# Dropping TensorE's constant multiplications from a 256-token, six-FFN network in split fp32

## The chip, the cores and the metric

The kernel runs on one core of one Trainium2 chip. The metric is device time in microseconds, the median of several executions. A core has TensorE (PE: matmuls, and PEld for its weight loads), VectorE (DVE), ScalarE (ACT), GpSimd (POOL) and SyncE (SP), each with its own in-order queue, coupled by semaphores.

## The reference

Two networks in a row act on x of 256 tokens by 1024 features, all in fp32:

```python
# first_block, DEPTH = 2
for i in range(DEPTH):
    x = layer_norm(ALPHA * x + 0.5 * swiglu(x, ...), ...)
    x = layer_norm(ALPHA * x + (mixer_ab or mixer_c)(x, ...), ...)
    x = layer_norm(ALPHA * x + memory_attn(x, mem, ...), ...)
    x = layer_norm(ALPHA * x + 0.5 * swiglu(x, ...), ...)
# second_block, DEPTH = 2
for l in range(DEPTH):
    h = _rmsnorm(x, mix_norm[l])
    x = x + _mixer(h, ...)      # gated delta rule and HGRN2, both directions
    h = _rmsnorm(x, ffn_norm[l])
    x = x + _conv_ffn(h, ...)
return _rmsnorm(x, final_norm)
```

The mixer of the second block computes merged = sigmoid(gate_dn) * (o_dn @ w_branch_dn) + sigmoid(gate_hg) * (o_hg @ w_branch_hg), and returns merged @ w_out. The constant multiplications of the kernel appear nowhere in it.

## The kernel before, in words

All weights come in one stream of "units" of 128 x 2048 values (1 MB), by SP into a ring of three. ACT rounds each half unit to fp32r (w_hi, L1272), DVE (in some stages POOL, L2528) subtracts to get the rest (ring_lo, L1690), and PE multiplies three times: high by high, high by low, low by high. features (L714) makes one unit into one PSUM tile of two 128 x 256 halves, 48 matmuls with 256 moving columns (L724); tokens (L728) does the same with the roles exchanged; to_acc (L744) adds one unit into the four PSUM banks acc, 24 matmuls of 512 columns (L757). There are four rotating tile banks; open_tile (L687) waits until the bank's earlier tile was taken.

There are six FFNs, 0 to 3 in the first block, 4 and 5 in the second. A norm works on the finished acc banks: DVE adds them to x and takes statistics (L1769 and L1770, for RMS norms L2054 and L2055), ACT takes a square root, DVE normalizes the rows in two instructions (L1780, for RMS norms L2064; each adds 1 to the semaphore ln_xh), PE transposes them in 16 records (transposes, L772), ACT and DVE scale them out of PSUM, and ACT L1251 and DVE L1678 split them into xT_hi and xT_lo, which the first features wait for (await_x, L712). Norms 0 to 5 of the first block have two units of the memory's keys and values as work for PE (norm_filled, L817). The norm 6 before FFN 3 and the four RMS norms 0 to 3 go through norm_transposes (L806).

mixer2 (L1052) is run twice. After its projections come LEVELS + 2 = 9 levels (0 to 8): each has a gate unit (none at level 8), a wait for hg_k and hg_q (made by DVE L2214 and POOL L2559), and two tiles of 128 x 128 products (per_head, L1039). Then come the sums for the l2 norms, the decay tables (ACT L1613), a wait for l2_inv ahead of four more tiles, the transposes, seven rounds of a block inverse, the recurrence, the products with the branch weights (branch, L1190, matmuls in L1201), and the output projection (out_proj, L833), whose first to_acc waits for the merged operand.

keep_warm (L693 to L697) multiplies the identity by 512 columns of the constant table, n times, into a bank that later work overwrites; nobody reads the product. Its calls stand in norm_transposes (five times, L807), in out_proj (twice, L835), at level 0 (five times) and level 8 (four times, L1072), before l2_inv (three times, L1114) and before branch_dn (twice, L1210). Each of the five calls stands in PE's order just ahead of a wait. out_proj is used by the second block alone; so the places that are run are 5 norms, and 5 in each of the two layers' mixers.

Of the kernel before, what the change touches and what calls it, by code (L numbers as in the profile page):

```python
# [56 lines left out]
LEVELS = 7  # L57
# [400 lines left out]
def build(nc, weights, x_in, mem_in, consts, cols, ln_g_rows, ln_b_rows, gains, sink, rpb, hmask_in, wba_in, head_rows, decay_rows, final_norm,  # L458
          out):
    plan = Plan()  # L460
    with ExitStack() as ctx:
        def sb(name, shape, dt=F32):
            return ctx.enter_context(nc.sbuf_tensor(name, shape, dt))
# [16 lines left out]
        const = sb("const", [P, CONSTANTS_W])  # L480
# [41 lines left out]
        def table(name):  # L522
            a, n = CONSTANTS[name]
            return const[:, a:a + n]

        ident = table("ident")
# [19 lines left out]
        acc = [ctx.enter_context(nc.psum_tensor(f"acc{b}", [P, 512], F32)) for b in range(4)]  # L546
# [137 lines left out]
        def _(pe):  # L684
            mm = nc.tensor.matmul

            def open_tile(t, more=0):  # L687
                if t >= NB:

                    pe.wait_ge(tile_taken[t % NB], more + t // NB)  # L690
                return bank[t % NB]

            def keep_warm(ps, n):  # L693


                for _ in range(n):
                    mm(ps[:, :], ident, const[:, 0:512], start=True, stop=True)  # L697

            THREE = ((0, 0), (0, 1), (1, 0))
            x2 = (xT_hi, xT_lo)  # L700
            mem2 = (mem_hi, mem_lo)
# [12 lines left out]
            def features(u, t, x_set=None, more=0, x2=x2):  # L714

                for f in range(2):
                    w = open_half(u, f, KT, more)
                    if f == 0:
                        ps = open_tile(t, more)
                    for k in range(KT):  # L720
                        if x_set is not None and f == 0 and k % 2 == 0:
                            await_x(x_set, k // 2)
                        for i, (a, b) in enumerate(THREE):
                            j = mm(ps[:, f * S:(f + 1) * S], w[a][:, k, :], x2[b][:, k, :],  # L724
                                   start=(k == 0 and i == 0), stop=(k == KT - 1 and i == 2))
                    j.then_inc(sems["unit_used" if f else "half_used"], 1)
# [38 lines left out]
            def transposes(t0, src):  # L765

                for q in range(4):
                    ps = open_tile(t0 + q)
                    for k in range(2):
                        for tt in range(TT):  # L770
                            c = (2 * q + k) * P
                            i = nc.tensor.transpose(ps[:, k * S + tt * P:k * S + (tt + 1) * P],  # L772
                                                    src[:, tt, c:c + P], ident)
                    i.then_inc(sems["tile_ready"], 1)

            def await_features(t0):
                for q in range(4):
                    pe.wait_ge(*taken(t0 + q))
# [24 lines left out]
                    transposes(plan.tile["mem"], mem_rows)  # L803
                down(FT // 2 - 1, u0 + FU - 1, False, True)

            def norm_transposes(key, inst, warm=5):  # L806
                keep_warm(open_tile(plan.tile[key]), warm)  # L807
                pe.wait_ge(sems["ln_xh"], 2 * (inst + 1))
                transposes(plan.tile[key], xh)
                await_features(plan.tile[key])  # L810
# [17 lines left out]
            def out_unit(n, j):  # L828

                await_x(("out", n), j)  # L830
                to_acc(plan.unit[("out", n, j)], x2, 2 * j, j == 0, j == 3)

            def out_proj(n):  # L833

                keep_warm(acc[0], 2)  # L835
                for j in range(4):
                    out_unit(n, j)

# [180 lines left out]
            norm_filled(5)  # L1019
            memory_attention(1)  # L1020
            norm_transposes(("ln", 6), 6)
            ffn(3, ("ln", 6))

# [11 lines left out]
            def per_head(t, lhsT, rhs, part=lambda out: out):  # L1035

                ps = open_tile(t)
                for h in range(4):
                    i = mm(part(ps[:, h * P:(h + 1) * P]), lhsT(h), rhs(h), start=True, stop=True)  # L1039
                i.then_inc(sems["tile_ready"], 1)  # L1040

            def hd(h):
                return slice(h * P, (h + 1) * P)

            def turn4(t, src):

                ps = open_tile(t)
                for b in range(4):
                    i = nc.tensor.transpose(ps[:, b * P:(b + 1) * P], src(b), ident)
                i.then_inc(sems["tile_ready"], 1)  # L1050

            def mixer2(l):  # L1052
                U, T = plan.unit, plan.tile
# [14 lines left out]
                for i in range(LEVELS + 2):  # L1068
                    if i < 8:
                        features(U[("gate", l, i)], T[("gate", l, i)])  # L1070
                    if i in (0, LEVELS + 1):
                        keep_warm(open_tile(T[("level", l, i)]), 5 if i == 0 else 4)  # L1072
                    pe.wait_ge(sems["hg_k"], (LEVELS + 2) * l + i + 1)
                    pe.wait_ge(sems["hg_q"], (LEVELS + 2) * l + i + 1)
                    K, Q = hKQ[:, i % 2, 0], hKQ[:, i % 2, 1]
                    for c in range(2):
                        s, t = (c, c) if i <= LEVELS else (c, 1 - c)
                        per_head(T[("level", l, i)] + c,
                                 lambda h: K[:, h * S + s * P:h * S + (s + 1) * P],
                                 lambda h: Q[:, h * S + t * P:h * S + (t + 1) * P])  # L1080

                pe.wait_ge(sems["l2_sq"], 4 * l + 4)
                ps = open_tile(T[("l2", l)])
                for c in range(16):
                    i = mm(ps[:, c:c + 1], l2s[:, c // 2, (c % 2) * P:(c % 2 + 1) * P], table("ones")[:, 0:1],  # L1085
                           start=True, stop=True)
# [4 lines left out]
                for tt in range(TT):  # L1091
                    ps = open_tile(T[("hg_o", l)] + tt)
                    for h in range(4):
                        for st in range(TT):
                            i = mm(ps[:, hd(h)], hatt[:, st, h, tt * P:(tt + 1) * P], hi[:, st, hd(h)],  # L1095
                                   start=(st == 0), stop=(st == TT - 1))
# [3 lines left out]
                ps = open_tile(T[("gcum", l)])  # L1100
# [5 lines left out]
                i = mm(ps[:, 16:32], table("ones"), gg[:, :], start=True, stop=True)  # L1106
# [4 lines left out]
                             lambda h: gg[:, tt * 8 + d * 4 + h:tt * 8 + d * 4 + h + 1].to_broadcast([P, P]),  # L1111
                             lambda h: sums[d])

                keep_warm(acc[0], 3)  # L1114
                pe.wait_ge(sems["l2_inv"], l + 1)
                for j in range(4):
                    per_head(T[("l2B", l)] + j, lambda c: l2i[:, 4 * j + c:4 * j + c + 1].to_broadcast([P, P]),
# [64 lines left out]
                for tt in range(TT):  # L1182
                    pe.wait_ge(*taken(T[("QK", l)] + tt))
                    ps = open_tile(T[("dn_o", l)] + tt)
                    for h in range(4):
                        for d in range(2):
                            i = mm(ps[:, hd(h)], qkd[:, 2 * tt + d, hd(h)], vn[:, 2 * tt + d, hd(h)],  # L1187
                                   start=(d == 0), stop=(d == 1))
                    i.then_inc(sems["tile_ready"], 1)
                def branch(name, q0):  # L1190

                    for j in range(2):
                        for half in range(2):
                            w = open_half(U[(name, l)] + j, half, 4)
                            ps = open_tile(T[(name, l)] + 2 * j + half)
                            for f in range(2):
                                for k in range(4):
                                    if j + half + f == 0 and k % 2 == 0:
                                        await_x(("branch", l), q0 + k // 2)
                                    for p, (c, d) in enumerate(THREE):  # L1200
                                        i = mm(ps[:, f * S:(f + 1) * S], w[c][:, k, f * P:(f + 1) * P],  # L1201
                                               x2[d][:, 2 * q0 + k, :], start=(k + p == 0), stop=(k == 3 and p == 2))
                            i.then_inc(sems["unit_used" if half else "half_used"], 1)
# [3 lines left out]
                pe.wait_ge(sems["dn_out"], l + 1)  # L1207
                for j in range(2):
                    turn4(T[("dn_T", l)] + j, lambda b: dn_o[:, b % 2, hd(2 * j + b // 2)])
                keep_warm(acc[0], 2)  # L1210
                branch("branch_dn", 2)
                out_proj(4 + l)

            pe.wait_ge(sems["head_in"], 16 * 2)
            for l in range(DEPTH):
                norm_transposes(("rms", 2 * l), 8 + 2 * l)
                mixer2(l)
                norm_transposes(("rms", 2 * l + 1), 9 + 2 * l)
                ffn(4 + l, ("rms", 2 * l + 1))
# [1412 lines left out]
```

## Time and profile before

| | |
|---|---|
| median of 3 runs | 2501.81 us (2498.66 to 2504.06) |
| the profiled execution | 2507.15 us |
| its span, first to last instruction | 2505.3 us |
| mean granted TensorE clock | 0.963 |
| PE busy | 2325.2 us, 93% |
| DVE busy | 1661.1 us, 66% |
| ACT busy | 1057.3 us, 42% |
| DMA | 359.80 MB, mean 144 GB/s |

The clock is given as a share of full speed: 1.00 is 2.4 GHz, 0.50 is 1.2 GHz. In a timeline row the columns are start, duration, engine, line and operation, then output and inputs; a bracket tells how long the engine was idle before it and who ended that. Each fp32 matmul with fp32 operands appears as two records; those of the three-part products (fp32r) appear as one. The ends of PE's records are modelled, so neighbours overlap; their starts are the better measure.

### The profile page before, as it was taken

The numbers are of one execution on the slowest core, as the hardware profiler recorded it, in microseconds if no ns is written. First come the engines' busy times: TensorE is split into PE (matmuls) and PEld (weight loads), VectorE is DVE, ScalarE is ACT, GpSimd is POOL, SyncE is SP. The second block draws the span as 40 slices with busy tenths as digits, with TensorE's granted clock in tenths as the row PEclk, the third lists the DMA queues.
The fourth block names the chain that finished last, engine by engine and source line by source line (L and its number), as shares of the span: only waits on it lengthen the run. The fifth ranks groups of instructions, "written<-read, shape, count | busy, mean of one in ns | idle before, by whom it ended". The sixth has DMA issues, their size and how long they took to land. (4 is left out here: it accounts for less than half of the span.)

```text
span 2505.3 us, 40714 instructions
## 1 busy us (share of the span) xinstructions
PE 2325.2 (93%) x16414; PEld 2162.1 (86%) x16414; DVE 1661.1 (66%) x2425; ACT 1057.3 (42%) x1481; POOL 309.2 (12%) x192
## 2 busy tenths in 40 slices
PE   7999789989999999999979887999999887899997
PEld 7999659879999997989969877988998887897997
DVE  4557656665665567665567886467666988547766
ACT  4335445433443456543335444234444443324432
POOL 0000000320000000000003353400000544320000
PEclk9999889989999999999989898999999998899999
DMA  6555314755455543445535320024554332003553
GB/s 258 187 186 178 109 48 155 189 180 185 178 201 187 188 161 120 158 153 186 186 119 185 119 100 34 1 89 164 185 184 165 139 117 85 1 18 144 187 184 132
DMA packets 52674, 359.80 MB, mean 144 GB/s; under 512 B 6401, under 2 KB 6785, under 8 KB 10945
## 3 DMA queue, kind: packets, MB, share of 16 engines
q1 hardware_dynamic: 46928, 340.81, 37.9%
q0 software_dynamic: 4336, 13.37, 1.9%
q10 hardware_dynamic: 1280, 3.77, 0.4%
q8 instruction: 97, 1.59, 0.3%
q14 instruction: 33, 0.26, 0.0%
HBM read 356.88 MB, written 1.05 MB: 143 GB/s over the span
## 5 line engine op out<-in xcount | busy, mean ns | idle before, releaser
L1690 DVE TENSOR_TENSOR ring_lo<-ring,w_hi 128x1024 fp32r<-128x1024 f32 x600 | 758.0, 1294 | 616.4 <-ACT w_hi L1272 614.7
L1272 ACT ACTIVATE w_hi<-ring 128x1024 fp32r<-128x1024 f32 x648 | 656.2, 1052 | 875.7 <-DMA ring<-weights 726.2
L724 PE MATMUL tile<-xT_hi,w_hi 128*128 128x256 f32 x3008 | 863.1, 287 | 38.3 <-DVE ring_lo L1690 24.4
L724 PE MATMUL tile<-xT_lo,w_hi 128*128 128x256 f32 x3008 | 858.7, 285 | 0.0
L724 PE MATMUL tile<-xT_hi,ring_lo 128*128 128x256 f32 x3008 | 858.3, 285 | 0.0
L724 PEld LDWEIGHTS tile<-xT_hi,w_hi 128*128 128x128 f32 x3008 | 585.4, 195 | 45.5 <-DVE ring_lo L1690 30.9
L724 PEld LDWEIGHTS tile<-xT_lo,w_hi 128*128 128x128 f32 x3008 | 585.5, 195 | 2.1
L724 PEld LDWEIGHTS tile<-xT_hi,ring_lo 128*128 128x128 f32 x3008 | 584.7, 194 | 0.0
L1039 PE MATMUL tile<-work 128*128 128x128 f32 (+1 forms) x1600 | 201.1, 290 | 43.9 <-DVE work L2214 40.5
L1039 PEld LDWEIGHTS tile<-work 128*128 128x128 f32 x1600 | 195.5, 204 | 51.7 <-DVE work L2214 45.8
L757 PE MATMUL acc<-w_hi,hidden_hi 128*128 128x512 f32 x528 | 208.1, 394 | 5.7 <-DVE ring_lo L1690 5.6
L1237 ACT ACTIVATE work<-tile 128x512 f32<-128x512 f32 (+1 forms) x204 | 112.6, 574 | 228.3 <-PE tile L1039 120.0
L757 PE MATMUL acc<-w_hi,hidden_lo 128*128 128x512 f32 x528 | 207.5, 393 | 0.0
L757 PE MATMUL acc<-ring_lo,hidden_hi 128*128 128x512 f32 x528 | 206.6, 391 | 0.0
L2528 POOL TENSOR_TENSOR ring_lo<-ring,w_hi 128x1024 fp32r<-128x1024 f32 x48 | 133.8, 2797 | 469.6 <-ACT w_hi L1272 469.6
L757 PEld LDWEIGHTS acc<-w_hi,hidden_hi 128*128 128x128 f32 x528 | 100.2, 190 | 26.0 <-issue 6.0
L2502 POOL DMA_DIRECT2D work<-ln_g_rows x8 | 4.4, 555 | 937.1 <-DVE x L1791 936.8
L757 PEld LDWEIGHTS acc<-ring_lo,hidden_hi 128*128 128x128 f32 x528 | 99.9, 189 | 21.5
L757 PEld LDWEIGHTS acc<-w_hi,hidden_lo 128*128 128x128 f32 x528 | 100.1, 190 | 18.4
L737 PE MATMUL tile<-w_hi,xT_hi 128*128 128x256 f32 x352 | 102.5, 291 | 5.0 <-DVE work L1914 2.8
L737 PE MATMUL tile<-w_hi,xT_lo 128*128 128x256 f32 x352 | 101.9, 290 | 0.0
L737 PE MATMUL tile<-ring_lo,xT_hi 128*128 128x256 f32 x352 | 101.7, 289 | 0.0
(259 smaller groups left out, 3027.5 us busy)
## 6 DMA issues: line engine op xcount, KB each, us to landing
ring<-weights SPq DMA_DIRECT2D x324, 1024.0 KB, 4.8
work<-ln_g_rows POOLq DMA_DIRECT2D x8, 512.0 KB, 5.5
work<-ln_b_rows POOLq DMA_DIRECT2D x8, 512.0 KB, 6.7
work<-rpb POOLq DMA_DIRECT2D x32, 96.0 KB, 14.0
work<-hmask_in ACTq DMA_DIRECT2D x1, 1408.0 KB, 9.9
x<-x_in SPq DMA_DIRECT2D x1, 1024.0 KB, 8.0
work<-mem_in ACTq DMA_DIRECT2D x1, 1024.0 KB, 7.0
out<-x POOLq DMA_DIRECT2D x1, 1024.0 KB, 4.4
```

Of the source, the lines that this page charges most:

```text
L724: j = mm(ps[:, f * S:(f + 1) * S], w[a][:, k, :], x2[b][:, k, :], start=(k == 0 and i == 0), stop=(k == KT - 1 and i == 2))
L737: j = mm(ps[:, tt * 256:(tt + 1) * 256], x2[b][:, k, tt * P:(tt + 1) * P], w[k // 4][a][:, k % 4, :], start=(k == 0 and i == 0), stop=(k = ...
L757: j = mm(acc[b][:, :], src[d][:, at + k, (b // 2) * P:(b // 2 + 1) * P], w[k][c][:, 0, (b % 2) * 512:(b % 2 + 1) * 512], start=(first and ...
L1039: i = mm(part(ps[:, h * P:(h + 1) * P]), lhsT(h), rhs(h), start=True, stop=True)
L1237: A(dst, ps[:, :] if src is None else src(ps), ACT.Copy).then_inc(tile_taken[t % NB], 1)
L1272: A(high_of(u, h), half_of(ring, u, h), ACT.Copy).then_inc(sems["w_hi"], 1)
L1690: V.tensor_tensor(half_of(ring_lo, u, h), half_of(ring, u, h), high_of(u, h).bitcast(F32), ALU.subtract).then_inc(sems["w_lo"], 1)
L2502: pool.dma_start(g_rows, ln_g_rows[inst:inst + 1, :].partition_broadcast(P)).then_inc(sems["rows_in"], 16)
L2528: G.tensor_tensor(half_of(ring_lo, u + 2, h), half_of(ring, u + 2, h), high_of(u + 2, h).bitcast(F32), ALU.subtract).then_inc(sems["w_lo_p ...
```

## The change

The function keep_warm and its five calls are removed; the parameter warm of norm_transposes goes with them. Nothing else is changed.

```diff
-            def keep_warm(ps, n):
-
-
-                for _ in range(n):
-                    mm(ps[:, :], ident, const[:, 0:512], start=True, stop=True)
-
...
-            def norm_transposes(key, inst, warm=5):
-                keep_warm(open_tile(plan.tile[key]), warm)
+            def norm_transposes(key, inst):
                 pe.wait_ge(sems["ln_xh"], 2 * (inst + 1))
                 transposes(plan.tile[key], xh)
                 await_features(plan.tile[key])
...
             def out_proj(n):
 
-                keep_warm(acc[0], 2)
                 for j in range(4):
                     out_unit(n, j)
...
                     if i < 8:
                         features(U[("gate", l, i)], T[("gate", l, i)])
-                    if i in (0, LEVELS + 1):
-                        keep_warm(open_tile(T[("level", l, i)]), 5 if i == 0 else 4)
                     pe.wait_ge(sems["hg_k"], (LEVELS + 2) * l + i + 1)
...
-                keep_warm(acc[0], 3)
                 pe.wait_ge(sems["l2_inv"], l + 1)
...
                 for j in range(2):
                     turn4(T[("dn_T", l)] + j, lambda b: dn_o[:, b % 2, hd(2 * j + b // 2)])
-                keep_warm(acc[0], 2)
                 branch("branch_dn", 2)
                 out_proj(4 + l)
```

## Rows read from the trace of the kernel before

**Rows 1.** The page: the span, busy time of engines, and TensorE's granted clock in 40 slices.
```profile
span 2505.3 us, 40714 instructions
...
PE 2325.2 (93%) x16414; PEld 2162.1 (86%) x16414; DVE 1661.1 (66%) x2425; ACT 1057.3 (42%) x1481; POOL 309.2 (12%) x192
...
PEclk9999889989999999999989898999999998899999
```
**Rows 2.** Groups by line, PE: record count | busy us, mean ns | idle before.
```profile
L697 PE MATMUL tile<-const 128*128 128x512 f32 x86 | 38.4, 592 | 0.0
...
L697 PE MATMUL acc<-const 128*128 128x512 f32 x28 | 13.0, 592 | 0.0
```
**Rows 3.** Timeline at norm 6, before FFN 3: start, duration, engine, line.
```profile
1087.25 4.45 PE L697 MATMUL tile<-const 128*128 128x512 f32 x10
...
1089.93 1.53 DVE L1780 TENSOR_SCALAR work<-work,mv,rstd 128x1024 f32<-128x1024 f32 x2
...
1091.54 1.95 PE L772 MATMUL tile<-const,work 128*128 128x128 f32 x16
...
1095.53 0.35 PE L724 MATMUL tile<-xT_hi,w_hi 128*128 128x256 f32 x1 [2.04 <-DVE xT_lo L1678]
```
**Rows 4.** Timeline of PE at RMS norm 1, before FFN 4 (the second RMS norm).
```profile
1699.24 4.45 PE L697 MATMUL tile<-const 128*128 128x512 f32 x10
1703.92 1.97 PE L772 MATMUL tile<-const,work 128*128 128x128 f32 x16 [0.22 <-DVE work L2064]
1707.71 0.35 PE L724 MATMUL tile<-xT_hi,w_hi 128*128 128x256 f32 x1 [1.83 <-DVE xT_lo L1678]
```
**Rows 5.** Timeline of PE in layer 0's levels: behind gate unit 1, and level 8.
```profile
1467.33 2.98 PE L1039 MATMUL tile<-work 128*128 128x128 f32 x15 [4.36 <-DVE work L2214]
...
1529.32 1.01 PE L1039 MATMUL tile<-work 128*128 128x128 f32 x3 [6.34 <-DVE work L2214]
```
**Rows 6.** Timeline of PE behind the wait for l2_inv, layer 0.
```profile
1550.06 1.13 PE L1039 MATMUL tile<-const,small 128*128 128x128 f32 x8 [0.98 <-ACT work L1613]
...
1551.72 1.16 PE L1039 MATMUL tile<-const,small 128*128 128x128 f32 x8 [0.53 <-ACT work L1613]
```
**Rows 7.** Timeline of PE at branch_dn and at out_proj, layer 0.
```profile
1662.03 0.36 PE L1201 MATMUL tile<-xT_hi,w_hi 128*128 128x256 f32 x1 [0.62 <-DVE xT_lo L1678]
...
1677.35 0.50 PE L757 MATMUL acc<-w_hi,xT_hi 128*128 128x512 f32 x1 [1.85 <-DVE xT_lo L1678]
```
**Rows 8.** Stretches: us, busy (count) of PE, PEld, DVE, ACT, POOL; PEclk; DMA.
```profile
1096.10:1099.30 3.20, 3.20 (x17) 3.20 (x16) 3.20 (x4) 2.01 (x3) 0.00 (x0) 0.50 0.02 5
1101.10:1104.30 3.20, 3.20 (x29) 3.20 (x29) 3.17 (x4) 1.43 (x3) 0.00 (x0) 1.00 0.11 20
1307.80:1308.80 1.00, 0.00 (x0) 0.01 (x1) 1.00 (x3) 1.00 (x3) 0.00 (x0) 1.00 0.00 0
1386.00:1387.90 1.90, 0.00 (x0) 0.00 (x0) 1.90 (x5) 1.86 (x2) 0.75 (x1) 1.00 0.42 78
1389.60:1392.80 3.20, 3.20 (x17) 3.20 (x17) 3.17 (x9) 0.00 (x0) 0.61 (x1) 0.50 0.23 90
1396.00:1399.50 3.50, 0.00 (x0) 0.00 (x0) 3.28 (x7) 0.71 (x2) 0.00 (x0) 1.00 0.60 250
1399.80:1403.00 3.20, 2.88 (x13) 2.88 (x14) 3.09 (x8) 1.51 (x2) 1.61 (x1) 0.50 0.03 13
1705.95:1707.70 1.75, 0.00 (x0) 0.02 (x1) 1.67 (x4) 1.75 (x5) 0.00 (x0) 1.00 0.00 0
1707.80:1894.00 186.20, 186.20 (x1317) 175.51 (x1318) 135.52 (x206) 78.66 (x92) 0.00 (x0) 1.00 0.50 181
```
**Rows 9.** Timeline of PE at RMS norm 0, the first, before the mixer of layer 0.
```profile
1303.48 3.67 PE L772 MATMUL tile<-const,work 128*128 128x128 f32 x16 [15.17 <-DVE work L2064]
1308.82 0.36 PE L724 MATMUL tile<-xT_hi,w_hi 128*128 128x256 f32 x1 [1.66 <-DVE xT_lo L1678]
```
**Rows 10.** Source view of line 2064: duration ns min/median/max, first and last start.
```profile
L2064 DVE TENSOR_SCALAR work<-x,rstd x10: 748/751/754, 1302.0 to 2494.8; 128x1024 f32<-128x1024 f32 x10
```

## The prediction

> **What bounds the kernel now.** I read the page first. TensorE (PE) is busy for 93% of a span of 2505.3 us, and its clock row stands at eight or nine tenths throughout [rows 1]. So PE sets the end, and the clock it is granted matters. The profiled execution took 2507.15 us, 1.85 more than its span and 5.3 more than the median of the runs, 2501.81. All terms below are differences within that execution, so I add their sum to either.
>
> Next come the groups by line for what goes away: 86 + 28 records, 38.4 + 13.0 = 51.4 us of busy time, no idle ahead of them [rows 2]. Two records make one fp32 multiplication, so 57 multiplications go, at 0.90 us each. The tempting sum takes 51.4 us off the end. Whether any of it comes off depends, at each place, on what the next PE instruction waits for. So I read the timeline at all 15 places: five norms with transposes of their own, and five in each of the two mixers.
>
> At the norm before FFN 3 the ten records start at 1087.25; VectorE's (DVE's) normalization of both row halves ends at 1089.93 + 1.53 = 1091.46; the transposes start at 1091.54 [rows 3]. At the second RMS norm 0.22 us of idle even stand between the filler and the transposes, ended by DVE L2064 [rows 4]. The next two RMS norms read the same within 0.25 us. In the mixer the idle left behind the fillers is 6.34 us at level 8 [rows 5], 0.98 at l2 [rows 6], and 0.62 at branch_dn and 1.85 at out_proj [rows 7], the same in both layers. Everywhere the release comes last, not the filler.
>
> **The change part by part.** *PE work removed.* The gain per place is the filler's end less the release, at most the 0.1 us of rows 3: nothing in all. What hides this work is the wait itself. The wait inside open_tile that some fillers took is made again by the first transpose or per_head, so no wait moves and nothing queues differently behind one. No DMA and neither SP's nor POOL's queue is touched.
>
> *What follows a silent PE.* Without fillers PE is idle from where they start to the next start: 4.3 us before FFN 3 [rows 3], 4.7 at the second RMS norm [rows 4] (4.4 and 4.7 at the next two). Elsewhere it is the idle left plus 0.90 per multiplication: 3.7 us at l2 (three), 2.4 at branch_dn (two), 3.7 at out_proj (two), about 10 at level 8. The stretches show what such idle brings [rows 8]. After 1.9 us of idle from 1386.0 the next 3.2 us stand at a granted clock of 0.50, that is 1.2 GHz; after 3.5 us of idle from 1396.0 again; after the 2.04 us of idle behind FFN 3's transposes [rows 3] again, at 1096.1. After 1.75 us of idle from 1705.95 FFN 4 ran its 186 us at 1.00 (2.4 GHz). Every idle stretch that the change makes is longer than those 1.9 and 2.04.
>
> *The price of the lower clock.* Of features, 17 fall in 3.2 us at 0.50 and 29 at 1.00 [rows 8]. By these counts such a stretch costs 3.2 x (1 - 17/29) = 1.3 us, by the clock's ratio 1.6; I take 1.5. Sixteen transposes take 3.67 us when PE comes out of a long idle [rows 9] and 1.97 at 1.00 [rows 4]. To the first feature behind them it is 1308.82 - 1303.48 = 5.34 us against 1707.71 - 1703.92 = 3.79, so 1.55 us more. Nothing later absorbs this in an FFN: PE is busy 186.20 of 186.20 us there [rows 8].
>
> *The sum by place.*
> - Norm before FFN 3: its features pay for one slow stretch already; new are slow transposes, 1.5 us (0 to 3).
> - Three RMS norms: slow transposes, 1.55, and part of a stretch of features, up to 1.5. The nearest row, 3.5 us of idle, left the clock low for the first 3.2 us of work, and slow transposes last 3.67, so most is paid there: 2.5 each, 7.5 us (1.55 to 3.05 each).
> - Two branch_dn, idle 2.4, nearest the 1.9 with a fall: 1.5 each, 3.0 us (0 to 3 each).
> - Two out_proj, idle 3.7, nearest the 3.5: 1.5 each, 3.0 us (0 to 3 each).
> - Two l2, idle 3.7: the fall is as likely, but PE then goes in step with ACT, with idle ended by ACT L1613 ahead of each group of eight [rows 6], which absorbs a part; the transposes behind are exposed. 1.0 each, 2.0 us (0 to 4 each).
> - Level 0, two: nothing. Behind the next gate unit PE idles 4.36 us for DVE L2214 [rows 5], and that covers it; without the cover, 1.5 each.
> - Level 8, two, and the first RMS norm: nothing. The idle left there now, 6.34 [rows 5] and 15.17 us [rows 9], brings the clock down before PE resumes.
>
> Sum: 1.5 + 7.5 + 3.0 + 3.0 + 2.0 = 17.0 us. The profiled execution would come to 2524 us, the median to **2519 us**. Late next is whatever PE does behind each place, FFN 4 and 5 above all.
>
> *A rule against the rows.* At the first RMS norm the sixteen transposes were PE's only work since 15.17 us of idle [rows 9], and at 1307.8, before the features began, the clock stood at 1.00 again [rows 8]. So transposes bring it back, and I charge the norms for little behind them.
> The Trainium skill, "TensorE: Matmul & The Clock Gate", Part 4 (PE-mode transpose), says the opposite: in transpose mode the full clock does not engage, since it doesn't count as PE work in the same way. By it each of four norms would pay a further stretch of features. By that rule the third rival follows; this trace disagrees where it shows it.
>
> **The rivals.**
> 1. *No change.* The falls land in idle, or PE's lateness is hidden by what it waits for next. For it: before FFN 3 the clock fell in spite of the fillers [rows 3, 8]. Against it: behind the second RMS norm it did not fall, and there fillers are PE's only work in 4.7 us [rows 4, 8]. With 1 us at each of three RMS norms and nothing else: +3, 2505 us.
> 2. *Faster: the fillers slow the chains that PE waits for.* The place is DVE's and ACT's work beside the fillers, 51.4 us of it; the mechanism, that PE's reads and writes of memory hold theirs up. If those chains grew shorter by a share s, s x 51.4 us comes off: over 33% beats the clock's 17 us, and with the +3 of rival 1, over 6% decides. Against it: the ten executions of DVE's L2064 took 748 to 754 ns, with fillers beside them or not [rows 10]. With a share of 20% and +3: 2495 us.
> 3. *Dearer: the clock comes back late.* The features behind four norms start slow too, 1.5 more each (6 us), and each of the six other places pays two stretches, 3.0 in place of 1.5 or 1.0 (10 us). In all 17 + 16 = 33; with half of the second part, +28, 2530 us. Against it: the row at 1307.8 [rows 8], and that after the slow stretches of rows 8 the rows come back to 1.00 at 1101.1.
> 4. *The change doesn't do what it says:* left aside, since the function and its five calls all go.
>
> **How the numbers follow.** The forecast's case, +6 to +26, gets 0.78, no change (rival 1) 0.09, faster 0.03, dearer than +26 0.10. The range's low end is the sum with branch_dn, out_proj and l2 at nothing and the RMS norms at 1.55 each: 1.5 + 4.65 = +6. The high end is rival 3: +28. That is 2508 to 2530 us. A measurement of this kernel can tell about 0.2%, 5 us, from no change. Slower by more than that gets 0.88, within it 0.09, faster 0.03.
>
> **What would show it right or wrong.** Right: the work behind each wait starts as far behind PE's last work as now (4.3, 4.7, 2.4 and 3.7 us); the transposes of the three RMS norms take 3 to 3.7 us for 16; stretches at 0.50 stand at those places; the mean granted clock falls by some 0.01; the FFNs stay without idle, each starting later. Wrong: if those transposes still take 1.97 us and what is behind them runs at 1.00 (rival 1); if the statistics ahead of L2064 get shorter (rival 2); if features are slow for over 3 us behind slow transposes (rival 3).

## The result, and the profile after

| | before | changed |
|---|---|---|
| median, 7 runs each | 2502.95 us | 2514.74 us |
| ratio | | 1.0049, 95% interval 1.0034 to 1.0065 |
| profiled execution's span | 2505.3 us | 2512.9 us |
| mean granted TensorE clock | 0.963 | 0.952 |
| PE busy | 2325.2 us | 2286.8 us |

The change costs 12.3 us (8.5 to 16.3). PE is busy for 38 us less, and the kernel ends later. A second build of the same changed kernel gave 1.0067 (1.0053 to 1.0081). Microseconds given with a ratio are that ratio less 1, times the median of the kernel before.

These are the page's lines that answer to [rows 1]:

```profile
span 2512.9 us, 40485 instructions
...
PE 2286.8 (91%) x16300; PEld 2153.2 (86%) x16300; DVE 1658.7 (66%) x2425; ACT 1058.6 (42%) x1481; POOL 306.2 (12%) x192
...
PEclk9999889999999999999989888999999988899999
```

PE's other 16300 records are there in both traces in the same order, so a start can be compared with its counterpart. (All line numbers after the removed function are lower now: L766 was L772, L718 was L724, L751 was L757, L1190 was L1201, L1031 was L1039, L2052 was L2064.) The timeline of PE at norm 6, at RMS norms 1 and 2, and at branch_dn and out_proj of the layers 0 and 1, answers to [rows 3, 4, 7]:

```profile
1087.04 3.01 PE L766 MATMUL tile<-const,work 128*128 128x128 f32 x16 [4.11 <-DVE work L1768]
1091.83 0.55 PE L718 MATMUL tile<-xT_hi,w_hi 128*128 128x256 f32 x1 [1.78 <-DVE xT_lo L1666]
...
1660.88 0.36 PE L1190 MATMUL tile<-xT_hi,w_hi 128*128 128x256 f32 x1 [2.33 <-DVE xT_lo L1666]
...
1677.69 0.50 PE L751 MATMUL acc<-w_hi,xT_hi 128*128 128x512 f32 x1 [3.57 <-DVE xT_lo L1666]
...
1705.88 3.47 PE L766 MATMUL tile<-const,work 128*128 128x128 f32 x16 [4.51 <-DVE work L2052]
1711.00 0.35 PE L718 MATMUL tile<-xT_hi,w_hi 128*128 128x256 f32 x1 [1.66 <-DVE xT_lo L1666]
...
1902.50 2.70 PE L766 MATMUL tile<-const,work 128*128 128x128 f32 x16 [4.28 <-DVE work L2052]
1906.86 0.55 PE L718 MATMUL tile<-xT_hi,w_hi 128*128 128x256 f32 x1 [1.66 <-DVE xT_lo L1666]
...
2278.62 0.50 PE L751 MATMUL acc<-w_hi,xT_hi 128*128 128x512 f32 x1 [3.57 <-DVE xT_lo L1666]
```

The idle in the brackets took the place of the fillers to the tenth of a microsecond: at RMS norm 1 the transposes started 4.90 us behind the last acc matmul before and do so now. But they last 3.47 us instead of 1.97, and from their start to the first feature it is 5.12 us instead of 3.79. What the clock did is in the stretches (us; busy and count of PE, PEld, DVE, ACT, POOL; PEclk; DMA):

```profile
1088.00:1091.70 3.70, 2.04 (x10) 1.64 (x8) 2.72 (x7) 3.22 (x7) 0.00 (x0) 0.50 0.00 0
1091.90:1097.20 5.30, 5.30 (x25) 5.30 (x26) 5.30 (x7) 2.32 (x3) 0.00 (x0) 0.50 0.02 3
...
1661.30:1664.50 3.20, 3.20 (x17) 3.20 (x16) 1.18 (x2) 0.00 (x0) 0.00 (x0) 0.50 0.19 77
1678.40:1681.60 3.20, 3.20 (x9) 2.49 (x8) 3.20 (x4) 1.20 (x2) 0.00 (x0) 0.50 0.02 8
1705.70:1708.90 3.20, 3.02 (x14) 3.02 (x15) 2.13 (x4) 1.00 (x3) 0.00 (x0) 0.50 0.01 3
1709.10:1897.80 188.70, 187.04 (x1322) 176.09 (x1321) 137.81 (x209) 80.75 (x96) 0.00 (x0) 1.00 0.50 178
1903.70:1910.30 6.60, 4.94 (x24) 4.57 (x23) 5.87 (x10) 5.14 (x9) 0.00 (x0) 0.50 0.00 0
2259.90:2273.90 14.00, 11.67 (x98) 11.46 (x97) 9.12 (x12) 5.68 (x8) 0.00 (x0) 1.00 0.43 151
```

PE works at 1.2 GHz (0.50) behind nearly every wait that the fillers had covered. At branch_dn of layer 1 (2259.90) the clock stayed at 1.00, though PE had been idle just as long (2.33 us) as at that of layer 0.

The table below is worked out from the traces of all kernels that lack some fillers, as differences of start times: the first column is a part's length in the kernel before, the others how much longer it is. The kernels are described in the next section; **bold** marks a part whose own fillers are missing. "2nd" is a second trace of the same kernel (experiment 10).

| part | before, us | changed | changed, 2nd | norms only | branch and out only | levels and l2 only | all but levels and l2 | before, 2nd |
|---|---|---|---|---|---|---|---|---|
| start to norm 6 (nothing changed) | 1078 | -4.4 | -4.1 | -4.8 | -6.0 | -4.5 | -3.9 | -2.3 |
| norm 6: transposes to first feature | 3.99 | **+0.80** | **+1.17** | 0.01 | **+0.80** | **+1.39** | 0.00 | 0.00 |
| FFN 3, first 14.5 us | 14.52 | **+1.22** | **-1.50** | -1.49 | **+1.22** | **0.00** | 0.00 | -1.49 |
| RMS norm 0: 16 us of features | 16.26 | **+1.47** | **+0.01** | +2.65 | **+1.46** | **+1.42** | 0.00 | +1.42 |
| both layers, level 0 to the l2 products | 218 | **-1.1** | **-2.6** | **-1.6** | **-2.4** | +2.2 | **-2.4** | -1.0 |
| of these, level 0's products to level 1's | 18.35 | **+1.07** | **+1.21** | **+1.65** | **+1.34** | 0.01 | **+1.26** | -0.03 |
| l2 wait and what follows, layer 0 | 24.97 | **+0.01** | **0.00** | **+0.01** | **0.00** | -0.01 | **0.00** | 0.00 |
| branch_dn, layer 0 | 11.46 | **+1.50** | **+1.49** | **+1.49** | 0.01 | **+1.49** | 0.01 | 0.01 |
| branch_dn, layer 1 | 11.47 | **-0.01** | **+1.48** | **+1.48** | -0.01 | **+1.49** | -0.01 | 0.00 |
| out_proj, layer 0 | 21.67 | **+1.62** | **+1.60** | **+1.60** | 0.04 | **+2.41** | 0.04 | 0.04 |
| out_proj, layer 1 | 21.71 | **+1.58** | **+1.57** | **+1.55** | -0.04 | **0.00** | -0.04 | -0.04 |
| RMS norm 1: transposes to first feature | 3.79 | **+1.33** | **+1.37** | 0.00 | **+1.30** | **+1.50** | 0.00 | 0.00 |
| RMS norm 2: transposes and 17 us behind | 20.77 | **+2.12** | **+4.17** | 0.01 | **+1.55** | **+2.83** | 0.01 | 0.02 |
| RMS norm 3: transposes and 14 us behind | 17.79 | **+1.28** | **+1.38** | -0.01 | **+3.38** | **+3.22** | -0.01 | -0.01 |

RMS norm 0's features and the levels as a whole vary as much with their fillers (+1.42 and +2.65; +2.2) as without. Level 0 by itself doesn't: in the five traces without its five multiplications level 1 begins 1.1 to 1.65 us later, both layers together, and in the two others it moves by 0.03 at most. Without them the stretch at half clock there lasts longer (1439.90 to 1446.60 at 0.50 in experiment 4, against 1447.60 to 1450.80 in the kernel before). The other bold parts of the first trace of the changed kernel add up to 0.80 + 1.22 + 0.01 + 1.50 - 0.01 + 1.62 + 1.58 + 1.33 + 2.12 + 1.28 = 11.45 us, nearly the 12.3 of the medians. With level 0's 1.07 they make 12.5. The spans differ by only 7.6, because parts far ahead of the change happened to take 4.4 us less.

### The profile page after: what moved, and what is told of

It reads as the page before. It is cut to its first block and busy times, and to the rows that moved or that the text cites. A ratio compares the mean times of both kernels' runs of the same rounds, so it can differ in the third digit from the quotient of the medians.

```text
span 2512.9 us, 40485 instructions
## 1 busy us (share of the span) xinstructions
PE 2286.8 (91%) x16300; PEld 2153.2 (86%) x16300; DVE 1658.7 (66%) x2425; ACT 1058.6 (42%) x1481; POOL 306.2 (12%) x192
## 3 DMA queue, kind: packets, MB, share of 16 engines
q8 instruction: 96, 1.57, 0.2%
## 5 line engine op out<-in xcount | busy, mean ns | idle before, releaser
L1678 DVE TENSOR_TENSOR ring_lo<-ring,w_hi 128x1024 fp32r<-128x1024 f32 x600 | 742.6, 1268 | 623.3 <-ACT w_hi L1260 621.6
L718 PE MATMUL tile<-xT_hi,w_hi 128*128 128x256 f32 x3008 | 865.3, 288 | 40.3 <-DVE ring_lo L1678 27.1
L718 PE MATMUL tile<-xT_lo,w_hi 128*128 128x256 f32 x3008 | 860.7, 286 | 0.0
L718 PE MATMUL tile<-xT_hi,ring_lo 128*128 128x256 f32 x3008 | 860.3, 286 | 0.0
L718 PEld LDWEIGHTS tile<-xT_hi,w_hi 128*128 128x128 f32 x3008 | 587.8, 195 | 48.0 <-DVE ring_lo L1678 33.8
L718 PEld LDWEIGHTS tile<-xT_lo,w_hi 128*128 128x128 f32 x3008 | 587.7, 195 | 2.1
L718 PEld LDWEIGHTS tile<-xT_hi,ring_lo 128*128 128x128 f32 x3008 | 587.1, 195 | 0.0
L1031 PE MATMUL tile<-work 128*128 128x128 f32 (+1 forms) x1600 | 202.9, 291 | 60.3 <-DVE work L2202 56.6
L1031 PEld LDWEIGHTS tile<-work 128*128 128x128 f32 x1600 | 197.9, 206 | 65.0 <-DVE work L2202 59.0
L751 PE MATMUL acc<-w_hi,hidden_hi 128*128 128x512 f32 x528 | 206.6, 391 | 3.9 <-DVE ring_lo L1678 3.9
L751 PE MATMUL acc<-w_hi,hidden_lo 128*128 128x512 f32 x528 | 206.2, 390 | 0.0
L751 PE MATMUL acc<-ring_lo,hidden_hi 128*128 128x512 f32 x528 | 205.5, 389 | 0.0
L751 PEld LDWEIGHTS acc<-w_hi,hidden_hi 128*128 128x128 f32 x528 | 99.4, 188 | 23.8 <-issue 4.2
L751 PEld LDWEIGHTS acc<-ring_lo,hidden_hi 128*128 128x128 f32 x528 | 99.2, 188 | 21.2
L751 PEld LDWEIGHTS acc<-w_hi,hidden_lo 128*128 128x128 f32 x528 | 99.4, 188 | 18.3
```

Source lines behind the costliest of these rows:

```text
L751: j = mm(acc[b][:, :], src[d][:, at + k, (b // 2) * P:(b // 2 + 1) * P], w[k][c][:, 0, (b % 2) * 512:(b % 2 + 1) * 512], start=(first and ...
L1678: V.tensor_tensor(half_of(ring_lo, u, h), half_of(ring, u, h), high_of(u, h).bitcast(F32), ALU.subtract).then_inc(sems["w_lo"], 1)
```

## The experiments

All are made from the kernel before, and compared with it on the same chip, except where the text says otherwise. Ratios are to the kernel before.

**1. Fillers at the norms only.** The calls in out_proj, at the levels, before l2_inv and before branch_dn go.

```diff
-                keep_warm(acc[0], 2)
                 for j in range(4):
                     out_unit(n, j)
...
-                    if i in (0, LEVELS + 1):
-                        keep_warm(open_tile(T[("level", l, i)]), 5 if i == 0 else 4)
...
-                keep_warm(acc[0], 3)
                 pe.wait_ge(sems["l2_inv"], l + 1)
...
-                keep_warm(acc[0], 2)
                 branch("branch_dn", 2)
```

> The 25 constant multiplications of the five norms stay, the 32 of the mixers go. Clock theory: the transposes of norm 6 and of RMS norms 1 to 3 take 1.95 to 2.0 us for 16 again; slow stretches stand behind branch_dn of at least one layer and behind both starts of out_proj, 1.5 to 1.6 us each; sum +3 to +6 us over the kernel before. No-change theory: within 2 us of the kernel before. Theory that fillers slow their neighbours: the mixers' DVE and ACT chains get shorter and the time falls below the kernel before.

Measured: 1.0016 (1.0007 to 1.0025), so +4.0 us (1.8 to 6.3). The table has it at branch_dn (1.49, 1.48) and out_proj (1.60, 1.55), 6.1 us in this trace, with the norms' own parts as before.

**2. Fillers before branch_dn and in out_proj only.**

```diff
-                keep_warm(open_tile(plan.tile[key]), warm)
...
-                    if i in (0, LEVELS + 1):
-                        keep_warm(open_tile(T[("level", l, i)]), 5 if i == 0 else 4)
...
-                keep_warm(acc[0], 3)
                 pe.wait_ge(sems["l2_inv"], l + 1)
```

> Fillers stay before branch_dn and in out_proj alone (8 multiplications). Clock theory: +5 to +9 us over the kernel before, all of it in the transposes and first features of norm 6 and RMS norms 1 to 3 (1.3 to 2.1 us each); the first acc matmuls of out_proj start 0.23 us apart. The other theories: +0 to 2 us.

Measured: 1.0047 (1.0034 to 1.0060), +11.8 us: more than expected. The places are those expected, and out_proj and branch_dn are clean; but RMS norm 3 paid 3.38 us, since its features were slow too, and its norms add up to 8.25 us in this trace, norm 6 and its features being 2.02 of them. Against the usual start of FFN 3 with fillers, which is 1.49 us shorter than in the first trace of the kernel before (see the columns with a plain -1.49), it is 9.7.

**3. Fillers at the levels and l2 only.**

```diff
-                keep_warm(open_tile(plan.tile[key]), warm)
...
-                keep_warm(acc[0], 2)
                 for j in range(4):
...
-                keep_warm(acc[0], 2)
                 branch("branch_dn", 2)
```

> Fillers stay at levels 0 and 8 and before l2_inv alone (24 multiplications, 21.6 us of PE work). Clock theory, as the trace of the changed kernel has it: these gain nothing, so the time is that of the changed kernel, +10 to +14 us over the kernel before. Theory of my forecast, l2 at 1.0 us each: 2 us less than that. Theory that fillers slow their neighbours: more than the changed kernel, by up to a share of 21 us.

Measured: 1.0058 (1.0044 to 1.0072), +14.5 us (11.0 to 18.0), just over the 10 to 14 expected. The 21.6 us of fillers in these places gain nothing that the times can tell.

**4. All but the levels and l2**, the counterpart of 3:

```diff
-                    if i in (0, LEVELS + 1):
-                        keep_warm(open_tile(T[("level", l, i)]), 5 if i == 0 else 4)
...
-                keep_warm(acc[0], 3)
                 pe.wait_ge(sems["l2_inv"], l + 1)
```

> The kernel before without the fillers of levels 0 and 8 and of l2 alone (24 of 57 multiplications). My forecast: l2 at 1.0 us each, levels at nothing: +2 us. By the traces so far, in which l2 and what follows it lasts the same to 0.02 us with and without fillers, and the levels scatter by 3 us either way: 0 us, within 3. If the levels, being on the path, do pay for the missing fillers, +3 to +5 us.

Measured: 1.0004 (0.9996 to 1.0013), +1.0 us (-1.0 to +3.3): 24 of the 57 multiplications can go at a price of 3 us at most. The trace has 1.26 us of it at level 0 (see the table), and nothing at l2. There the clock does fall without them. The stretch of the changed kernel and the timeline of PE and ACT in it:

```profile
1548.70:1551.90 3.20, 3.00 (x14) 3.03 (x15) 0.83 (x2) 3.02 (x11) 1.86 (x2) 0.50 0.02 5
```

```profile
1548.90 4.58 PE L1031 MATMUL tile<-const,small 128*128 128x128 f32 x24 [3.56 <-ACT work L1601]
1549.38 1.12 ACT L1601 ACTIVATE work<-tile,small 128x128 f32<-128x128 f32 x4
...
1551.14 1.13 ACT L1601 ACTIVATE work<-tile,small 128x128 f32<-128x128 f32 x4
...
1554.07 1.16 PE L1031 MATMUL tile<-const,small 128*128 128x128 f32 x8 [0.60 <-ACT work L1601]
```

ACT starts its groups of four 1.75 to 1.76 us apart in both kernels. The slow PE runs 24 records through where before it stopped for ACT ahead of each eight [rows 6], and by 1554 it waits for ACT again.

**5. Twice the fillers at the norms.** This measures what the waits cover.

```diff
-            def norm_transposes(key, inst, warm=5):
+            def norm_transposes(key, inst, warm=10):
```

> Ten multiplications in place of five at each of the five norms: 9 us of fillers against waits of 4.3 to 4.9 us (19.6 at RMS norm 0). What waits cover and what lies beyond: the transposes of norm 6 and RMS norms 1 to 3 start 8.55 to 8.6 us behind the last acc matmul, 3.7 to 4.3 us later than before, 15 to 17 us in all, less up to 1.5 for a slow stretch that goes at norm 6: the time is 13 to 17 us over the kernel before. If PE's fillers were hidden by something else than the waits I name, nothing or another number.

Measured: 1.0055 (1.0039 to 1.0071), +13.8 us (9.8 to 17.8). From the last acc matmul to the transposes it took 4.29, 3.91, 4.14 and 3.91 us longer at norm 6 and RMS norms 1 to 3, 16.3 in all. FFN 3 has no slow stretch in this trace (-1.50), but neither has it in three traces with five multiplications (experiment 10). The timeline of PE at RMS norm 1:

```profile
1695.25 8.74 PE L697 MATMUL tile<-const 128*128 128x512 f32 x20
1703.83 1.91 PE L772 MATMUL tile<-const,work 128*128 128x128 f32 x16
```

Here no idle stands between fillers and transposes, where [rows 4] has 0.22 us: ten multiplications are the bound, five are not.

**6. More fillers everywhere**, at waits that still showed idle:

```diff
                 transposes(plan.tile[key], xh)
+                keep_warm(acc[0], 2)
                 await_features(plan.tile[key])
...
-                keep_warm(acc[0], 2)
+                keep_warm(acc[0], 4)
                 for j in range(4):
                     out_unit(n, j)
...
+                keep_warm(open_tile(t0), 14)
                 pe.wait_ge(sems["ab_roped"], 2)
...
-                    if i in (0, LEVELS + 1):
-                        keep_warm(open_tile(T[("level", l, i)]), 5 if i == 0 else 4)
+                    n_warm = {0: 8, 1: 4, 2: 3, 3: 1, LEVELS + 1: 10}.get(i, 0)
+                    if n_warm:
+                        keep_warm(open_tile(T[("level", l, i)]), n_warm)
...
-                keep_warm(acc[0], 3)
+                keep_warm(acc[0], 4)
                 pe.wait_ge(sems["l2_inv"], l + 1)
...
-                norm_transposes(("rms", 2 * l), 8 + 2 * l)
+                norm_transposes(("rms", 2 * l), 8 + 2 * l, 5 if l else 21)
```

> Fillers at more places, and longer ones, nowhere longer than the wait by the trace of before: 2 multiplications behind the transposes of each norm with transposes of its own, 21 in place of 5 at RMS norm 0, 14 before the wait for the roped rows of the first block, 4 in place of 2 in out_proj, 4 for 3 before l2_inv, 8, 4, 3, 1 at levels 0 to 3, 10 at level 8. Clock theory: slow stretches at norm 6, RMS norm 0 and the roped rows go, 1.5 us for each slow set of transposes or stretch of features, 3 to 8 us less than the kernel before; the levels give nothing. Theory that fillers slow their neighbours: slower than before, with 50 us more of them.

Measured: 0.9944 (0.9931 to 0.9956), -14.0 us: well over the 3 to 8 that I expected (and with 80 multiplications, 72 us, more than before, not the 50 us of my text), though the level numbers were put wrong. Besides levels 0 and 8, PE's idle of over 1 us stands at levels 2, 4 and 6, not at 1 to 3; the heading of [rows 5] and my sentence on it, "behind the next gate unit", have the same slip: that row is level 2's. So the two halves were tried apart.

**7. More in the levels only**, at the right ones:

```diff
-                    if i in (0, LEVELS + 1):
-                        keep_warm(open_tile(T[("level", l, i)]), 5 if i == 0 else 4)
+                    n_warm = {0: 8, 2: 4, 4: 3, 6: 1, LEVELS + 1: 10}.get(i, 0)
+                    if n_warm:
+                        keep_warm(open_tile(T[("level", l, i)]), n_warm)
```

> The kernel before with longer fillers in the levels alone: 8, 4, 3, 1 and 10 multiplications at levels 0, 2, 4, 6 and 8, where the traces show idle (26 in place of 9). My forecast, that lateness in the levels is hidden by the waits for DVE L2214: no change, within 2 us of the kernel before. Rival, from the trace of the kernel with more fillers everywhere: gate units at half clock hold up ACT, which holds up GpSimd and DVE, so the levels are on the path; 3 to 8 us less than the kernel before, in the stretches from level 0 to the l2 products.

Measured: 0.9962 (0.9949 to 0.9975), -9.5 us (6.3 to 12.8 less): my forecast of no change is out. From the start of level 0 to that of level 7 in layer 0 it takes 66.48 us in place of 71.53. The stretches over these levels, of this kernel and then of the kernel before:

```profile
1440.70:1507.50 66.80, 60.98 (x466) 56.03 (x466) 64.04 (x58) 25.16 (x24) 38.59 (x14) 1.00 0.27 95
```

```profile
1445.90:1517.60 71.70, 60.46 (x449) 59.45 (x450) 64.79 (x59) 24.89 (x24) 38.13 (x14) 0.90 0.24 89
```

The clock is at 1.00 throughout instead of 0.90, and POOL's waits for ACT shrink by 11.3 us (kernel before, then this one; waits in the levels of layer 0: us in total, times, longest us), though a wait of 4.9 us for PE L1039 is new:

```profile
POOL work L2559 <- ACT work L1587: 40.5, 7, 8.8
```

```profile
POOL work L2560 <- ACT work L1588: 29.2, 6, 5.8
```

So PE's speed in the gate units does reach the end. The way there is read from the program, and no run changed it alone: ACT takes each gate tile out of PSUM ahead of the next level's exponential, for which POOL and DVE wait.

In the same trace out_proj of layer 1 takes 1.56 us more, with its two fillers in place: the clock stood at 0.50 from 2258.10 to 2261.40, behind 1.85 us of idle. A filler of two multiplications makes the fall there rarer; it doesn't rule it out.

**8. More everywhere but in the levels:** experiment 6 with the levels as before.

```diff
                 transposes(plan.tile[key], xh)
+                keep_warm(acc[0], 2)
                 await_features(plan.tile[key])
...
-                keep_warm(acc[0], 2)
+                keep_warm(acc[0], 4)
                 for j in range(4):
                     out_unit(n, j)
...
+                keep_warm(open_tile(t0), 14)
                 pe.wait_ge(sems["ab_roped"], 2)
...
-                keep_warm(acc[0], 3)
+                keep_warm(acc[0], 4)
                 pe.wait_ge(sems["l2_inv"], l + 1)
...
-                norm_transposes(("rms", 2 * l), 8 + 2 * l)
+                norm_transposes(("rms", 2 * l), 8 + 2 * l, 5 if l else 21)
```

> The kernel before with more fillers everywhere but in the levels: 2 multiplications behind the transposes of the norms, 21 at RMS norm 0, 14 before the roped rows, 4 in out_proj, 4 before l2_inv. Clock theory: 1.5 us off at the transposes of RMS norm 0, 1.5 off at the features behind norm 6, up to 3 off in the attention behind the roped rows: 3 to 6 us less than the kernel before. If the levels are what gained in the kernel with more everywhere, this one gains little over 3.

Measured: 0.9979 (0.9968 to 0.9990), -5.3 us. Twenty-one multiplications ahead of RMS norm 0 turn its 3.67 us of transposes [rows 9] into 1.96:

```profile
1275.86 18.18 PE L697 MATMUL tile<-const 128*128 128x512 f32 x42
1295.45 1.96 PE L772 MATMUL tile<-const,work 128*128 128x128 f32 x16 [1.40 <-DVE work L2066]
```

The two halves, -9.5 and -5.3, add up to 14.8, near the 14.0 of experiment 6.

**9. Both (7 and 8), and the qkv projection.**

```diff
                 for j in range(6):
+                    keep_warm(acc[0], (0, 0, 1, 2, 5, 0)[j])
                     features(U[("qkv", l)] + j, T[("qkv", l)] + j)
```

> Fillers of the last two extended kernels together, and 1, 2 and 5 multiplications before the third to fifth unit of the qkv projection, where PE idles 1.3, 2.0 and 4.6 us for the weights' low part. Clock theory: at least the gain of the kernel with more everywhere (13.5 us less than before), and a slow stretch or two less per layer in the qkv projection, 15 to 20 us less than before. Against: the qkv stage waits for weights, so PE's speed there is hidden and only the first number comes.

Measured: 2485.61 us, 0.9929 (0.9916 to 0.9942), -17.8 us. Its trace has 2.8 us less in the projections of layer 0 and nothing less in those of layer 1. It is the fastest of all kernels here, 1.2% under the first build of the changed one.

**10. Both kernels again.** The changed kernel as it is, and the kernel before for one execution.

> The changed kernel once more, for a second look at which places pay: +12 us over the kernel before (8 to 16). By the clock theory the places are the same, each 1.3 to 3.5 us at norm 6 and RMS norms 1 to 3, 0 or 1.5 at branch_dn, 0 to 2.4 at out_proj, but not all the same number as in the first look.

> The kernel before once more, one look: if the slow stretches fall by chance, the parts that nothing was changed in (attention of the first block, start of FFN 1, levels) differ from the first look by 1 to 4 us, and norm 6 shows no slow stretch in its features, as in the four kernels that had its five multiplications.

Measured: 1.0067 (1.0053 to 1.0081) for the changed kernel, +16.8 us (13.3 to 20.3), where I expected 8 to 16; RMS norm 2 paid 4.17 us, more than the 3.5 I had allowed. The kernel before took 2503.89 us. The columns "2nd" are these two. As expected, FFN 3 of the kernel before began without a slow stretch this time. Of the five traces with five multiplications at norm 6 and none behind its transposes, two have that stretch (the first trace of the kernel before and experiment 4), three don't (its second, experiments 1 and 7).

## Why the prediction was right, and where it was off

The forecast of 2519 us (+17) held: the median is 2514.74, the second build's 2519.89, both in the range of 2508 to 2530, and slower. The mechanism is the one forecast: the waits hide the work that was removed, and the work behind them starts at half clock. That the second build meets 2519 almost exactly is in part luck, for the terms err in both directions and what happens at a place changes between executions; the bold parts of its trace, norm 6 to RMS norm 3 without the levels, add up to 12.7 us. Of the signs of being right, the mean granted clock fell by 0.011 (some 0.01 was named), and the transposes of the three RMS norms took 3.47, 2.70 and 3.40 us in the first trace (3 to 3.7 was named).

- *"Nothing" for the PE work removed*: shown. In both traces of the changed kernel the waits are as long as before, start to start: within 0.05 us at the four norms and 0.01 at l2, branch_dn and out_proj. Experiment 5 is the other side of it: beyond the waits each multiplication costs its full time.
- *Norm 6, 1.5 us*: 2.0 (0.80 + 1.22) and -0.3 (1.17 - 1.50) against the first trace of the kernel before. My step "its features pay for one slow stretch already" rested on a chance of that execution. Against the traces without that stretch the missing fillers cost 3.5 and 1.2 us.
- *Three RMS norms, 2.5 each*: 1.33, 2.12, 1.28 in the first trace and 1.37, 4.17, 1.38 in the second; with experiments 2 and 3 the mean of the twelve is 2.1. The part from the transposes to the first feature is 1.3 to 1.54 in eleven of them, near the 1.55 of [rows 4, 9], and 0.57 at RMS norm 2 in the first trace, where the transposes took 2.70 us and the clock fell only while they ran; the rest is features at half clock, at some of the places.
- *branch_dn and out_proj, 1.5 each*: 1.5 where the clock fell (13 of the 16 bold entries lie from 1.48 to 1.62, one is 2.41), 0 where it didn't (two). The size was right, its certainty wasn't. One detail of the reading: behind the 1.9 us of idle the half clock begins at 1389.6, 1.7 us after the idle ended [rows 8], and not with the first work.
- *l2, 1.0 each*: mis-sized; it is 0.01 us in layer 0 and 0.03 in layer 1 at most. The clock fell, but ACT L1601 paces PE there, and the transposes behind came after the clock had risen. This term is plainly wrong, 2 of the 17 us.
- *Levels and the first RMS norm, nothing*: near in size (experiment 4), but with a wrong reason. I took it that PE's lateness in the levels is hidden behind the wait for DVE L2214. Level 1 starts 1.1 to 1.65 us later without level 0's fillers, and experiment 7 shows how much of the levels the clock decides. The fillers of levels 0 and 8 matter so little because the clock falls in the levels with them as well: they stand at two of five idle places, and at level 0 it fell in spite of them, as this stretch of the kernel before has it:

```profile
1447.60:1450.80 3.20, 3.20 (x17) 3.20 (x17) 3.20 (x2) 0.00 (x0) 3.20 (x2) 0.50 0.00 0
```

The rivals. *No change* is out for the norms, branch_dn and out_proj, is true of l2, and nearly so of the levels. *Fillers slow their neighbours* is out: the chains beside them end at the same distance with and without, and the kernels with more of them, inside the waits, are faster. *Dearer* happened in single places, not everywhere: RMS norm 2 in the second trace (+4.17), and by the sign that I had named, features slow for over 3 us, also norm 6 and RMS norm 2 in the first (0.50 until 1097.20, with features from 1091.83, and until 1910.30, with features from 1906.86). The rule named for it, that transposes don't count towards the full clock (the Trainium skill, "TensorE: Matmul & The Clock Gate", Part 4), is again not what the trace shows: at RMS norm 1 the transposes alone came between 4.51 us of idle and the row 1709.10 with 1.00, before the features at 1711.00.

## What to carry to other kernels

Before removing work as useless, read what ends the wait behind it: here 51.4 us of it were hidden in waits, and its removal cost 12 us through a slower clock. A filler pays when PE's next work is on the path and the fall lands in that work; where another engine paces PE (l2) it did nothing, and where idle beside it brings the clock down anyway (levels 0 and 8) it did little, 1.1 to 1.65 us. List PE's idle stretches (the shortest named here with a fall behind it is 1.85 us, and idle of that length also passed without one), fill each to just short of its release, and measure groups of them apart: 96 multiplications more than the kernel before had, in places of idle, gave 0.7%.

## What had not been expected of the hardware

The same binary's slow stretches fall elsewhere from one execution to the next. Parts that nothing was changed in, up to norm 6, differ by up to 6.0 us between traces (of 1078), the levels with their fillers as they were by 5.6 (-3.4 us in experiment 5, +2.2 in experiment 3), and branch_dn of one layer costs 1.5 us or nothing with the same idle ahead of it. Out_proj of layer 1 cost nothing more without its fillers in experiment 3, and 1.56 us more with them in experiment 7. The traces were not all taken on one chip, but the scatter isn't the chip's: thirteen executions of the kernel before on a single one took 2499.95 to 2508.68 us at a mean clock of 0.961 to 0.967. So single traces are compared part by part and not by their spans: 2512.9 against 2505.3 would have given 7.6 us for an effect of 12. What decides where a fall lands was not tried.
